# Decoder step on one NeuronCore: key transposes in two row halves, attention values and decode outputs in four column groups, and a reordered first unit

## The reference

```python
x = x + 0.5 * swiglu(rmsnorm(x, norm_ffn1), ffn1_w_in, ffn1_w_out)    # 1024 -> 2*2816 -> 1024
p = rmsnorm(x, norm_mix) @ w_in_mix                                   # 1024 -> 3592
o_a, s_fin = hgrn2(a_q, a_f, a_i, a_g, lb, gain, state0)              # 4 heads, state 128x128
# fox_prompt, per head: causal softmax attention with a decay from cumulated log f
s = einsum('bqhd,bkhd->bhqk', qi, kf) + ci[..., None] - cum[:, :, None, :]
o = einsum('bhqk,bkhd->bqhd', softmax(s), vf)
# fox_decode, per sequence: the same over the paged cache
s_past = einsum('bqhd,bkhd->bhqk', qf, k_past) + cq[..., None] + suffix[:, :, None, :]
o = einsum('bhqk,bkhd->bqhd', p[..., :p_len], v_past) + ...
x = x + concatenate([o_a, headnorm(o_f)]) @ w_out_mix
x = x + 0.5 * swiglu(rmsnorm(x, norm_ffn2), ffn2_w_in, ffn2_w_out)
y = rmsnorm(x, norm_final)
```

## Time and profile before

| | |
|---|---|
| time, median of 3 runs | 1346.06 us (1345.54 to 1347.76) |
| time of the profiled execution | 1347.32 us |
| its span, first to last instruction | 1345.6 us |
| busy share of the span: PE, PEld, DVE, ACT, POOL | 97%, 90%, 45%, 34%, 8% |
| mean granted TensorE clock | 0.988 |
| read from HBM | 162.19 MB, 127 GB/s over the span |

### The profile page before, as it was taken

How to read it: one execution, slowest core, us unless ns; L and a number is a source line. 1 busy time by engine, 2 the same in 40 slices (tenths; PEclk the granted TensorE clock), 3 DMA queues, 4 the chain that set the end, 5 groups by cost and what they waited for, 6 DMA issues and landing times.

```text
span 1345.6 us, 27368 instructions
## 1 busy us (share of the span) xinstructions
PE 1308.5 (97%) x11235; PEld 1216.7 (90%) x11235; DVE 606.6 (45%) x1057; ACT 457.7 (34%) x710; POOL 102.6 (8%) x115
## 2 busy tenths in 40 slices
PE   6999999999999999989989999999999999999998
PEld 6999999999999999976657666589999999999997
DVE  5653432333454433347666566545533432334433
ACT  6343221222323113514536556634322221222322
POOL 1000000000022000004322100004000000000000
PEclk9999999999999999999989999999999999999998
DMA  7233422233322442156888887522333332233201
GB/s 189 68 94 94 137 83 62 63 94 101 101 93 64 116 134 86 39 171 225 275 290 300 330 313 263 170 90 68 94 94 94 118 101 62 63 94 101 87 31 66
DMA packets 192013, 172.17 MB, mean 128 GB/s; under 512 B 11393, under 2 KB 155298, under 8 KB 191938
## 3 DMA queue, kind: packets, MB, share of 16 engines
q1 hardware_dynamic: 191730, 170.61, 40.3%
q0 software_dynamic: 144, 0.52, 0.1%
q10 hardware_dynamic: 64, 0.02, 0.0%
HBM read 162.19 MB, written 8.93 MB: 127 GB/s over the span
## 4 chain that ended last, share of the span: by engine, by line
PE 92%; DVE 4%; issue 1%; DMA 1%; ACT 1%; SPq 0%; POOL 0%; DVEq 0%; ACTq 0%
PE ps L2018 74%; PE ps L968 3%; PE ps L1051 2%; PE ps L1070 2%; PE ps L932 1%; PE ps L903 1%; PE ps L741 1%; DMA w_raw<-in_ffn_w_in 1%; PE ps L859 1%; PE ps L920 1%; DMA d_keys<-in_cache_k 1%; PE ps L1037 0%; PE ps L2141 0%; PE ps L2156 0%; DVE w_lo L2346 0%
## 5 line engine op out<-in xcount | busy, mean ns | idle before, releaser
L2018 PE MATMUL ps<-n_hi,w_hi 128*128 128x272 f32 x1856 | 388.6, 289 | 6.4 <-DVE w_lo L2472 2.9
L2018 PE MATMUL ps<-n_hi,w_lo 128*128 128x272 f32 x1856 | 388.2, 289 | 0.0
L2018 PE MATMUL ps<-n_lo,w_hi 128*128 128x272 f32 x1856 | 386.8, 288 | 0.0
L2192 ACT ACTIVATE w_hi<-w_raw 128x2048 fp32r<-128x2048 f32 (+2 forms) x77 | 157.8, 2050 | 540.0 <-PE ps L2018 540.0
L2018 PEld LDWEIGHTS ps<-n_hi,w_hi 128*128 128x128 f32 x1856 | 294.5, 189 | 7.0 <-issue 6.8
L2018 PEld LDWEIGHTS ps<-n_lo,w_hi 128*128 128x128 f32 x1856 | 294.2, 189 | 0.0
L2018 PEld LDWEIGHTS ps<-n_hi,w_lo 128*128 128x128 f32 x1856 | 292.3, 190 | 0.0
L2346 DVE TENSOR_TENSOR w_lo<-w_raw,w_hi 128x2048 fp32r<-128x2048 f32 (+2 forms) x77 | 196.2, 2548 | 48.7 <-ACT w_hi L2192 48.7
L2018 PE MATMUL ps<-g_hi,w_lo 128*128 128x272 f32 x704 | 145.7, 288 | 0.0
L2018 PE MATMUL ps<-g_hi,w_hi 128*128 128x272 f32 x704 | 145.6, 288 | 0.0
L2018 PE MATMUL ps<-g_lo,w_hi 128*128 128x272 f32 x704 | 145.1, 288 | 0.0
(11 more groups left out here) (348 smaller groups left out, 1224.8 us busy)
## 6 DMA issues: line engine op xcount, KB each, us to landing
w_raw<-in_ffn_w_in SPq DMA_DIRECT2D x87, 512.0 KB, 5.0
d_keys<-in_cache_k SPq DMA_DIRECT2D x128, 256.0 KB, 4.7
d_values<-in_cache_v SPq DMA_DIRECT2D x124, 256.0 KB, 5.3
w_raw<-in_w_in_mix SPq DMA_DIRECT2D x28, 512.0 KB, 4.8
w_raw<-in_ffn_w_out SPq DMA_DIRECT2D x16, 768.0 KB, 5.4
w_raw<-in_ffn_w_out SPq DMA_DIRECT2D x16, 640.0 KB, 5.4
w_raw<-in_w_out_mix SPq DMA_DIRECT2D x8, 512.0 KB, 4.9
suffix_scratch<-d_log_f_sums SPq DMA_DIRECT2D x32, 64.0 KB, 2.1
```

Source lines behind the costliest of these rows:

```text
L2018: mm = pe.matmul(bank(4 * j + 2 * t + half), wp, xp[:, k, half * HALF:(half + 1) * HALF], start=(k == 0 and wp is w[0] and xp is x_hi), st ...
L2192: nc.scalar.activation(w_hi[j][:, 0:kt * UC], w_raw[j][:, 0:kt * UC], ACT.Copy).then_inc(w_hi_ready, 1)
```

## The change

It has four parts.

1. **Key transposes in two row halves.** Each 128x128 transpose becomes two transposes of 64 positions, one from partitions 0 to 63 and one from 64 to 127, each with 64 moving columns. Half r goes to bank `B_KT + r`, so each bank now holds 64 positions of both strips, and `kT_done` is raised twice at the end of the sixteen. ACT waits for both before its first copy. The decode scores read the keys of two pages with a moving operand in two pieces for each page.
2. **Values of the prompt attention** move to `fox_values_tensor`, called after `outputs_tensor`, and each product with 128 stationary columns becomes four with 32, one for each column group.
3. **Decode outputs** in the same way: four products with 32 stationary columns for each of the four strips.
4. **The start.** Ten products of constants before the first transposes and seven after x 2; up columns loaded before token tiles 3 to 5, and split by ACT and DVE before these are copied; tile 5 has PSUM banks of its own.

```diff
+        def x_bank(i, q):
+            return 4 + 2 * (i % 2) + q if i < NX - 1 else 1 + 2 * q
...
+        HP = PAGE // 2
...
+        def fox_values_tensor(pe, x):
...
+                    for t in tiles:
+                        for s in range(t + 1):
+                            for g in range(4):
+                                rows = slice(g * NS, (g + 1) * NS)
+                                mm = pe.matmul(ps[rows, B_C, t * DH:(t + 1) * DH],
+                                               probT[u % 2][:, k * P + g * NS:k * P + (g + 1) * NS],
+                                               v_nat[:, s, h * DH:(h + 1) * DH], start=(s == 0), stop=(s == t),
+                                               skip_group_check=True)
+                            k += 1
+                    mm.then_inc(fpv_done, 1)
...
                 for m in range(SET_PAGES):
-                    mm = pe.transpose(ps[:, B_KT + k, m * PAGE:(m + 1) * PAGE], d_k[n % K_RING][:, m, j * P:(j + 1) * P],
-                                      ident[:, :])
-                mm.then_inc(kT_done, 1)
+                    for r in range(2):
+                        rows = slice(r * HP, (r + 1) * HP)
+                        mm = pe.transpose(ps[:, B_KT + r, (k * SET_PAGES + m) * HP:(k * SET_PAGES + m + 1) * HP],
+                                          d_k[n % K_RING][rows, m, j * P:(j + 1) * P], ident[rows, rows])
+                        if k == 1 and m == SET_PAGES - 1:
+                            mm.then_inc(kT_done, 1)
...
                     for j in range(NJ):
-                        mm = pe.matmul(ps[:, B_M, M_OUT + j * NR:M_OUT + (j + 1) * NR], d_o[:, j * P:(j + 1) * P],
-                                       d_w[c % 2][:, :], start=True, stop=True, skip_group_check=True)
+                        for g in range(4):
+                            mm = pe.matmul(ps[g * NS:(g + 1) * NS, B_M, M_OUT + j * NR:M_OUT + (j + 1) * NR],
+                                           d_o[:, j * P + g * NS:j * P + (g + 1) * NS], d_w[c % 2][:, :], start=True,
+                                           stop=True, skip_group_check=True)
...
+                    c0 = (k * SET_PAGES + 2 * q) * HP
+                    keys = d_kT[:, y % 2, :, c0:c0 + 2 * HP].rearrange("p r (m c) -> p m r c", c=HP)
...
+                act.wait_ge(kT_done, 2 * x + 2)
                 for k in range(2 if x < KEYS_BY_SCALAR else 1):
-                    act.wait_ge(kT_done, 2 * x + k + 1)
...
                     sp.dma_start(dst[:, :, 0:P], src[:, :, ds(tile * P, P)]).then_inc(w0_landed, 16)
-                    for i in range(3, NX):
-                        load_x(i)
                     for h in range(2):
                         ks = slice(h * KD // 2, (h + 1) * KD // 2)
                         sp.dma_start(dst[:, ks, P:UC], src[:, ks, ds(tile * P + D_FF, P)]).then_inc(w_landed[j], 16)
+                    for i in range(3, NX):
+                        load_x(i)
...
+            def keep_busy(n):
+                for _ in range(n):
+                    pe.matmul(ps[:, 3, 0:P], ones[:, :], ones[:, :], start=True, stop=True)
+
+            pe.wait_ge(const_ready, 1)
+            keep_busy(10)
             pe.wait_ge(const_ready, 2)
...
             for i in range(3):
                 transpose_x(i)
+            keep_busy(7)
```

More of the change, by code:

```diff
@@ L905, in fox_scores_tensor @@
                     c0 += (t + 1) * P
+        def fox_values_tensor(pe, x):
+            for u in range(UNITS):
+                h, r = divmod(u, 3)
+                tiles = UNIT_TILES[r]
+                if x == unit_at(u) + 3:
+                    pe.wait_ge(fpt_copied, u + 1)
+                    if r == 0:
+                        if h:
+                            pe.wait_ge(fo_scaled, 2 * h)
+                        else:
+                            pe.wait_ge(hfin, H_HG)
+                    k = 0
+                    for t in tiles:
[8 more added lines that the diff above has]
+                    mm.then_inc(fpv_done, 1)
         def fox_tensor(pe, x):
@@ L921, in fox_tensor @@
                     mm.then_inc(fpt_done, 1)
-                if x == unit_at(u) + 3:
-                    pe.wait_ge(fpt_copied, u + 1)
-                    if r == 0:
-                        if h:
-                            pe.wait_ge(fo_scaled, 2 * h)
-                        else:
-                            pe.wait_ge(hfin, H_HG)
-                    k = 0
-                    for t in tiles:
-                        for s in range(t + 1):
-                            mm = pe.matmul(ps[:, B_C, t * DH:(t + 1) * DH], probT[u % 2][:, k * P:(k + 1) * P],
-                                           v_nat[:, s, h * DH:(h + 1) * DH], start=(s == 0), stop=(s == t),
-                                           skip_group_check=True)
-                            k += 1
-                    mm.then_inc(fpv_done, 1)
             for j in range(NJ):
@@ L1050, in scores @@
                     g = 2 * half + q
+                    c0 = (k * SET_PAGES + 2 * q) * HP
+                    keys = d_kT[:, y % 2, :, c0:c0 + 2 * HP].rearrange("p r (m c) -> p m r c", c=HP)
                     mm = pe.matmul(ps[g * NR:(g + 1) * NR, B_S, pp * 2 * PAGE:(pp + 1) * 2 * PAGE],
-                                   d_q[b % 2][:, j * NR:(j + 1) * NR], d_kT[:, y % 2, k, q * 2 * PAGE:(q + 1) * 2 * PAGE],
-                                   start=(j == 0), stop=(j == NJ - 1), skip_group_check=True)
+                                   d_q[b % 2][:, j * NR:(j + 1) * NR], keys, start=(j == 0), stop=(j == NJ - 1),
+                                   skip_group_check=True)
                 mm.then_inc(qk_done, 1)
@@ L1101, in mix_tensor @@
                 outputs_tensor(pe, x)
+                fox_values_tensor(pe, x)
                 heads_tensor(pe, x)
@@ L1997, in transpose_x @@
                 for q in range(2):
-                    b = 4 + 2 * (i % 2) + q
-                    if i >= 2:
+                    b = x_bank(i, q)
+                    if 2 <= i < NX - 1:
                         pe.wait_ge(xt_copied[q], i - 1)
@@ L2271, in copy_x @@
                 act.wait_ge(xt_done, 2 * i + 2 + min(i, 1))
-                src = ps[:, 5 + 2 * (i % 2), :].rearrange("p (d c) -> p d c", c=P)[:, :, 0:X_N[i]]
+                src = ps[:, x_bank(i, 1), :].rearrange("p (d c) -> p d c", c=P)[:, :, 0:X_N[i]]
                 nc.scalar.activation(xT[:, 4:KD, X_ROW[i]:X_ROW[i + 1]], src, ACT.Copy).then_inc(xt_copied[1], 1)
@@ L2305, in _ @@
                 first_norm(0, range(k + 2, k + 4))
+            act.wait_ge(w_landed[0], 32)
+            nc.scalar.activation(up_columns(w_hi[0]), up_columns(w_raw[0]), ACT.Copy).then_inc(w_hi_ready, 1)
             for i in range(3, NX):
                 copy_x(i)
-            act.wait_ge(w_landed[0], 32)
-            nc.scalar.activation(up_columns(w_hi[0]), up_columns(w_raw[0]), ACT.Copy).then_inc(w_hi_ready, 1)
             first_norm(1, range(KD))
@@ L2451, in copy_x @@
                 dve.wait_ge(xt_done, 2 * i + 1 + min(i, 1))
-                src = ps[:, 4 + 2 * (i % 2), :].rearrange("p (d c) -> p d c", c=P)[:, :, 0:X_N[i]]
+                src = ps[:, x_bank(i, 0), :].rearrange("p (d c) -> p d c", c=P)[:, :, 0:X_N[i]]
                 nc.vector.tensor_copy(xT[:, 0:4, X_ROW[i]:X_ROW[i + 1]], src).then_inc(xt_copied[0], 1)
@@ L2474, in _ @@
                 first_norm(0, range(k + 2, k + 4))
-            for i in range(3, NX):
-                copy_x(i)
             dve.wait_ge(w_hi_ready, 1)
@@ L2479, in _ @@
                                     first_columns(w_hi[0], 1).bitcast(F32), ALU.subtract).then_inc(w_lo_ready, 1)
+            for i in range(3, NX):
+                copy_x(i)
             first_norm(1, range(KD))
```

## The result

The changed kernel takes 1326.03 us (median of 4 runs, 1324.6 to 1327.93) against 1346.05 (4 runs, 1345.54 to 1347.76): a ratio of 0.985, with a 95% interval of 0.9833 to 0.9867, so 20 us or 1.5% faster (interval 18 to 22 us). The forecast was 1320, its own band 1310 to 1328. The profiled execution took 1327.93, its span 1326.2, 19.4 less than before.

The account below looks back on a forecast made before the run. PE was taken to bound the mix stage through its chain of waits. From the profiled 1347.3 us, 21 (mix stage) and 5.3 (start) off gave 1321, against the median 1319.8, said as 1320; band 1310 to 1328 (0.62), range 1307 to 1338.

Parts of the forecast that it names:

- (a): Mix stage: the key transposes' row halves queue, 5 us lost instead of 16 won, 1341 or 1339 us; chance 0.14.
- (c): Key transposes: each change of row half drains PE, 0.15 us a transpose, 1399 us in all; chance 0.05.
- Key transposes, the share on the chain: Mix stage: of 24 us of PE saved on key transposes, two thirds lie on the chain of waits, giving 16 us.
- My signal for "wrong": Mix stage: evenly spaced transposes, new PE idle from DVE or d_keys past 10 us, or more windows at clock 0.5.
- rival (d): Mix stage: new waits eat the rest, DVE's chain takes over in most turns, gain 10 us, 1331 us; chance 0.10.
- the sum (21): Mix stage gain: 16 keys + 7.5 prompt values + 3.7 decode outputs - 4 shape changes - 2 transfers = 21 us.
- my own lower end of 14: Mix stage: the least gain expected, 14 us, if chains through DVE are right behind PE's.
- the 5.3: Start: constants at full clock and earlier up columns save 5.3 us, bounds 2.5 and 6.5.
- Transfers: Mix stage, turns 35 to 43: keys and values cannot come faster, so 2 us of gain are taken back.
- 7.5 + 3.7: Mix stage: gains on the chain from four column groups, 7.5 us for prompt values and 3.7 for decode outputs.
- Shape changes: Mix stage: 30 more changes of tile shape at 0.14 us each cost 4 us, all on the chain.
- Half clock (b): Mix stage: more half-clock stretches after PE waits, up to 3.5 us each; two give 1327, four 1334; chance 0.07.

Follow-up runs that it names:

- e2_keys: The kernel before with only the key transposes in two row halves: 1341.16 us, ratio 0.9955 to the kernel before.
- e9_fill: The changed kernel with 72 constant products filling PE's waits in the mix stage: 1327.77 us, ratio 0.9844 to the kernel before.
- e10_cold: The changed kernel without the constant products of the start, its order of the first unit kept: 1328.87 us, ratio 0.9857 to the kernel before.
- e12_fill_late: The changed kernel with first-half probability transposes behind the decode products and constant products in waits (none in turns 6 and 14): 1324.98 us.

## Why the prediction was right, and where it was off

**Key transposes, PE's share: right.** Pairs start some 3 ns apart and follow at 0.062 us; the block lost 0.33 us between first and last start, seven steps, where 0.38 was put for eight. (The prediction's (0.35 - 0.22) / 2 comes to 0.065, not 0.062; the starts themselves say 0.062.) The rival that row halves queue (a) and the rival that each change of half drains (c) are out. The rule of the Trainium skill that I held against this part ("TensorE: Matmul & The Clock Gate", section LDWEIGHTS), by which paired loads of 128 columns would need 0.86 us a turn by my estimate, is not what the trace has: 0.49. What Part 3 of that page says, that tiles in different row groups run together, the trace now shows, with their weight loads.

**Key transposes, the share on the chain: the step that was too large.** "On the chain stand 15.8% of 296 = 46.8 us of the 71.1 busy, two thirds, so 16 us", less 4 for shapes and 2 for transfers: 10. Measured alone it is 6.1 (2 us either way), on top of the other two parts 2.3 (some 4 either way). The share of a line in the chain of waits says how much of it was on the path, not how far the path shrinks before another takes its place. PE saved 27.3 us in the stage and 15.1 came back as waits: 3.6 for DVE, 3.3 for ACT, 3.2 for key pages and 5.0 for its own instructions. My signal for "wrong" named DVE lines and d_keys transfers only; these grew by 6.8 us, under its 10, and I had left ACT and the instruction supply out of it. For the stage the truth, 12.4, lies between rival (d) (10) and the sum (21), and below my own lower end of 14.

**The time is in the band partly by luck.** With the mix stage at 12.4 and the start at the 5.3 that I put, the time would be 1328.4, just outside. The start's 1.5 us more brought it in.

**Transfers: under-sized.** I took 2 us. The waits for d_keys rose by 3.2, and halving the values gave the changed kernel 3 us more than the kernel before, which alone is within the noise. The place was right: 3.7 us of them stand before the keys of turn 42, the rest before those of turn 44.

**Prompt values and outputs: right.** Value rounds follow at 0.056 us, as put. The time fell by 11.2 for 7.5 + 3.7, from 10.1 us less of PE (5.5 and 4.6) where I had 13.9. The values lost 7.6 us inside their blocks and gained 2.1 at the blocks' ends, where the next tile shape follows. Nearly all of the 10.1 came through, with less half clock besides: prompt values stand in turns 46 and on, where PE waited for 2.1 of 86 us before. That this is why is argued from the rows, not tried.

**Shape changes.** Where one tile shape follows another without a wait, the distance from start to start is longer than within the block before it. Summed over the mix stage that makes 32.7 us before (209 changes) and 35.5 after (234), 2.8 more. The 4 us were about right. The rule of the Trainium skill that a change of tiling mode drains the engine ("TensorEngine Tiling (Array Packing)", Key Properties) fits that.

**Half clock (b): small in the changed kernel, not in e2_keys.** In the changed kernel there are more stretches, six for three, another of my signals for "wrong", but they grew by 3.4 us only. With the keys alone they grew by 13.6, so a part of what this rival described may well stand in the 6.1 us of that part. What a stretch costs is not shown: a key transpose takes 57 ns from start to start in the mean at half clock and 32 at full clock, but the fill of e9_fill cost PE time itself.

**The start: 6.8 for 5.3.** The products came at full clock as put. The mis-sized term: "the second half of the gate columns is split by 15.1, before and after alike". DVE's timeline after:

```profile
10.82 0.69 DVE L2501 TENSOR_TENSOR w_lo<-w_raw,w_hi 128x512 fp32r<-128x512 f32 x1
...
13.09 0.68 DVE L2501 TENSOR_TENSOR w_lo<-w_raw,w_hi 128x512 fp32r<-128x512 f32 x1
```

That is 1.34 us earlier than 14.43, and the products followed at 17.87 instead of 18.9. Two things did it together. The gate columns landed sooner: ACT splits them at 10.18 without a wait, where before it waited for them until 11.51. And the constants that I had put down as a delay of 0.8 us brought the token transposes to full clock, so that the copies and norms ahead of the split came sooner. The sixteen transposes of token tiles 1 and 2, before and after:

```profile
7.25 2.93 PE L2002 MATMUL ps<-ident,x_nat 128*128 128x128 f32 x16
```

```profile
7.50 1.69 PE L2030 MATMUL ps<-ident,x_nat 128*128 128x128 f32 x16
```

e10_cold, with the new order of loads and without the constants, shows that the order alone does not move the split:

```profile
14.57 0.68 DVE L2499 TENSOR_TENSOR w_lo<-w_raw,w_hi 128x512 fp32r<-128x512 f32 x1
```

**Turns 44 to 63** were said to last 0.4 to 0.5 us less each. From turn 44 to 63 the changed kernel drew ahead by 5.3 us (from 4.51 to 9.80), 0.28 a turn, as three of the four instruction stalls lie there, in turns 48, 50 and 52, with 3.6 us. Without them it would be 0.47, by my estimate.

**The stage after the mix** was said to begin some 26 us earlier; it begins 19.2 earlier.

What stays open: how the 15 us of waits would split if each cause were taken away alone. The instruction stalls could be placed and named, but I made no version without them; that their 5 us are lost in the time was not tried. What half clock costs in either kernel is open too.

## What to carry to other kernels

A line's share of the chain of waits is not what a faster line gives: it says what was on the path, and another wait stood close behind. Where seven jobs hand work round, about half of what PE saved came through here. Before costing a saving, look for what the engine would meet if it came earlier: the next transfer (its landing time against the new turn), the next hand-over, and the instruction supply, if the saving is bought with more and shorter instructions. Test an extra such as keeping an engine busy on the kernel before too, and count what the extra costs: filling waits with constants was worth 4.3 us there and 0.8 after the change, though the other work fell by as much in both.

## What was not expected of the hardware

- Transposes in two row halves, 64 rows by 128 stationary columns of float32, start 3 ns apart with their weight loads, and a pair costs 0.062 us; one with 128 rows costs 0.110. Issued eight and eight, they still overlap by three.
- TensorE's instructions seem to come in 16 KB packets of some 128 matmul records with their loads (34 packets for 4239 records). Where many short ones follow each other, TensorE can stall in the middle of a block, for 0.5 to 1.7 us in the fourteen cases counted (2.2 once in e12_fill_late), and goes on 1.3 to 1.6 us after a packet that took 0.9 to 1.1 us has ended. In the kernel before, with 25 packets in 293 us, no such stall; with 34 in 280, four.
- Filling an engine's waits to keep its clock up has a price of its own. Ten constant products that ran at half clock took 4 us where the wait was 2.4, and 20.1 us of constants took away 13.7 us of waits in the changed kernel.
